# A hybrid decoder block on one core: five edits at the seams between its stages

## The reference

```python
z = rms_norm(h, norm_attn_g[i]) @ w_in[i]
y_attn = dilated_attention(q, k, v, rel_bias)
y_sgu = spatial_gating(z[..., o_g:o_s], ...)   # gelu, layer norm per group, causal 128x128 product, gate
y_ssm = s5_ssm(z[..., o_s:], ...)              # y = gelu(Re(C x) + D u); y * sigmoid(y @ glu_w + glu_b)
mix = concatenate([rms_scale(y_attn), rms_scale(y_sgu), rms_scale(y_ssm)], axis=-1) * branch_norm_g[i]
h = h + mix @ w_out[i]
h = h + conv_ffn(rms_norm(h, norm_ffn_g[i]), ...)   # up (width 5632), causal conv of 3, gelu(gate) * val, down
gate = sigmoid(rms_norm(h, norm_ple_g[i]) @ ple_w_gate[i])
h = h + gate * (p[i] @ ple_w_proj[i])
return rms_norm(h, final_norm_g)
```

## Time and profile before

| | |
|---|---|
| median of 3 runs | 2675.37 us (2674.75 to 2676.18) |
| profiled execution | 2676.85 us, span of its records 2675.3 us |
| mean granted PE clock | 0.973 of full |
| busy: PE, DVE, ACT, POOL | 95%, 67%, 51%, 31% |
| DMA | 420.97 MB, mean 157 GB/s |

### The profile page before, as it was taken

How to read it: one execution, slowest core, us unless ns; L and a number is a source line. 1 busy time by engine, 2 the same in 40 slices (tenths; PEclk the granted TensorE clock), 3 DMA queues, 4 the chain that set the end, 5 groups by cost and what they waited for, 6 DMA issues and landing times. The chain is left out here.

```text
span 2675.3 us, 38121 instructions
## 1 busy us (share of the span) xinstructions
PE 2532.1 (95%) x13395; PEld 2169.0 (81%) x13395; DVE 1794.4 (67%) x3337; ACT 1352.9 (51%) x2431; POOL 828.5 (31%) x625
## 2 busy tenths in 40 slices
PE   7999999999976899699999989999999999999998
PEld 6989979999965788488888868888888877887876
DVE  1113287777775776699999966879889975563333
ACT  4343424666645666455555546545555553444444
POOL 4454554655521111246555530002122210000000
PEclk9999999999987899799999999999999999999999
DMA  6675466788653454244444577543333336763221
GB/s 219 187 217 177 160 185 166 175 182 182 143 139 127 136 174 171 65 136 155 157 154 162 176 257 263 194 144 100 101 103 111 103 126 228 283 222 114 79 73 48
DMA packets 317450, 420.97 MB, mean 157 GB/s; under 512 B 31073, under 2 KB 229025, under 8 KB 312522
## 3 DMA queue, kind: packets, MB, share of 16 engines
q1 hardware_dynamic: 292090, 332.68, 41.4%
q0 software_dynamic: 25184, 86.01, 8.6%
HBM read 298.59 MB, written 124.16 MB: 158 GB/s over the span
## 5 line engine op out<-in xcount | busy, mean ns | idle before, releaser
L2834 PE MATMUL ffn_bank<-ffn_x,ffn_ring 128*128 128x512 f32 x704 | 278.1, 395 | 17.2 <-DVE ffn_strips L2632 8.9
L2836 PE MATMUL ffn_bank<-ffn_x,ffn_ring 128*128 128x512 f32 x704 | 277.2, 394 | 0.0
L2835 PE MATMUL ffn_bank<-ffn_x,ffn_ring 128*128 128x512 f32 x704 | 277.2, 394 | 0.0
L2908 POOL DMA_DIRECT2D ffn_act<-ffn_late x154 | 85.7, 558 | 476.1 <-DVE ffn_late L2664 445.4
L1203 POOL TENSOR_TENSOR in_w_lo<-in_w,in_w_hi 128x2048 fp32r<-128x2048 f32 x36 | 168.1, 4670 | 173.5 <-ACT in_w_hi L1071 173.5
L2834 PE MATMUL ffn_bank<-tail_shared,ffn_ring 128*128 128x512 f32 x528 | 206.3, 391 | 9.1 <-DVE ffn_ring L2607 7.5
L633 ACT ACTIVATE att_exps<-att_scores,att_part 128x256 f32<-128x256 f32 (+1 forms) x384 | 153.0, 454 | 105.1 <-DVE att_part L601 104.3
L2836 PE MATMUL ffn_bank<-tail_shared,ffn_ring 128*128 128x512 f32 x528 | 205.9, 390 | 0.0
L2431 ACT COPY ffn_strips<-ffn_bank 128x512 f32<-128x512 f32 x176 | 103.5, 588 | 147.6 <-PE ffn_bank L2836 147.6
L2648 DVE SCALAR_TENSOR_TENSOR ffn_strips<-ffn_strips,ffn_taps 128x512 f32<-128x512 f32 x176 | 144.6, 822 | 43.4 <-ACT ffn_strips L2446 43.4
L2834 PEld LDWEIGHTS ffn_bank<-ffn_x,ffn_ring 128*128 128x128 f32 x704 | 134.0, 190 | 49.0 <-issue 13.1
(11 more groups left out here) (441 smaller groups left out, 7369.3 us busy)
## 6 DMA issues: line engine op xcount, KB each, us to landing
ffn_w<-in_ffn_w_up SPq DMA_DIRECT2D x88, 512.0 KB, 4.8
ffn_act<-ffn_late POOLq DMA_DIRECT2D x154, 256.0 KB, 2.3
in_w<-in_w_in SPq DMA_DIRECT2D x36, 1024.0 KB, 6.6
ffn_a_raw<-ffn_act SPq DMA_DIRECT2D x77, 256.0 KB, 3.5
ffn_a_raw_later<-ffn_act SPq DMA_DIRECT2D x77, 256.0 KB, 4.4
ffn_w<-ffn_down_sums SPq DMA_DIRECT2D x16, 1024.0 KB, 5.1
ffn_w<-in_ffn_w_down SPq DMA_DIRECT2D x12, 1024.0 KB, 5.8
ffn_pieces<-in_ffn_w_down POOLq DMA_DIRECT2D x44, 256.0 KB, 3.6
```

Of the source, the lines that this page charges most:

```text
L2834: pe.matmul(out[:, :], hi[:, k], x_hi[kind][:, k], start=(k == 0 and fresh), stop=False, skip_group_check=not fresh)
L2835: pe.matmul(out[:, :], hi[:, k], x_lo[kind][:, k], start=False, stop=False, skip_group_check=not fresh)
L2836: mm = pe.matmul(out[:, :], lo[:, k], x_hi[kind][:, k], start=False, stop=(k == KH - 1), skip_group_check=not fresh)
```

## The change

1. `project_in`: the six bias bands are issued as before. Of the first head's twelve loads, the first half (six of 256 KB) is spread as four after block 29's work and two after block 30's, and the second half is cut in two parts of six smaller loads (128 KB each), spread over blocks 30, 31 and 32. The attention stage waits for 18 loads instead of 12.
2. `state_space`: the gate product `y @ glu_w + glu_b` is split by its contraction. The first half, with the bias written by a one-row matmul, is done in two batches of four banks, before q=4 and before q=6; ACT copies the banks to SBUF (`keep_first_glu`), DVE adds them to the second half later. `turn_y(0)` moves from q=6 to q=4. GpSimd multiplies three of the eight units (1, 3, 5). The load of mixing's row tile 0 is issued before the last store.
3. `mix_and_project`: ACT and DVE split weight chunk 0 ahead of waiting for row tile 0. In the opening step, `gate_product(3)` goes behind both products of tile 1, the turn of tile 2 behind it, and `gate_product(4)` from behind the products of tile 1 to behind the first products of tile 2.
4. `feed_forward`: the gain vector is loaded by SP near the end of the mixing stage. On ACT, PE and DVE the startup's pieces stand in another order, the second row group's turns have other banks, the copies of the first two products stand earlier, and the taps' turn and copy later.

The cut diff:

```diff
-                    load_first_head(0, units_to[G // 2 * NBLK] - 1)
+                if B == (G - 1) * NBLK + 2:
+                    load_first_head(0, 0, 4, units_to[G // 2 * NBLK] - 1)
+                if B == (G - 1) * NBLK + 3:
+                    load_first_head(0, 4, 6, units_to[G // 2 * NBLK] - 1)
+                    load_first_head(1, 0, 2, units_to[(G - 1) * NBLK] - 1)
+                if B == (G - 1) * NBLK + QK // WIDE:
+                    load_first_head(1, 2, 6, units_to[(G - 1) * NBLK] - 1)
                 if B == (G - 1) * NBLK + QK // WIDE + 1:
-                    load_first_head(1, units_to[(G - 1) * NBLK + QK // WIDE + 1] - 1)
+                    load_first_head(2, 0, 6, units_to[(G - 1) * NBLK + QK // WIDE] - 1)
             head_ahead.stored_counts = [stores_through(u) for u in range(U - RING, U)]
...
+    EARLY_AT, LATE_AT, EARLY_BANKS = Q // 2, Q - 2, 4
+    POOL_GATES = (1, 3, 5)
...
+                    if (h, l) == (HM - 1, L - 4):
+                        sp.wait_ge(stored[0], L // 4 * DMA)
+                        sp.dma_start(ahead.row0[:, heads * HEAD + GW:], mix[0:P, :]).then_inc(ahead.row0_loaded, DMA)
...
+            for n in POOL_GATES:
+                h, l = divmod(2 * n, L)
+                pool.wait_ge(rooted, n + 1)
+                nc.gpsimd.tensor_tensor(Y[:, h, l:l + 2, :], Y[:, h, l:l + 2, :], gate[:, h, l:l + 2, :], ALU.mult).then_inc(pool_out_ready, 1)
...
+            def first_glu_products(first):
+                for b in range(first, first + EARLY_BANKS):
+                    for i in range(2):
+                        n = 2 * b + i
+                        out = bank[b % EARLY_BANKS][:, i * W:(i + 1) * W]
+                        pe.matmul(out, ones[0:1, :], glu_b[0:1, :], start=True, stop=False)
+                        mm = pe.matmul(out, yT[:, 0, n * P:(n + 1) * P], glu_w[:, 0, :], start=False, stop=True)
+                    mm.then_inc(early_done, 1)
+
             for q in range(Q):
                 if q == MASK_AT:
                     turn_masks()
-                if q == Q - 2:
+                if q == EARLY_AT:
                     turn_y(0)
+                    pe.wait_ge(glu_loaded, 2 * DMA)
+                    pe.wait_ge(ones_ready, 1)
+                    pe.wait_ge(yT_copied, 4)
+                    first_glu_products(0)
+                if q == LATE_AT:
                     gate_product()
+                    pe.wait_ge(early_kept, EARLY_BANKS)
+                    first_glu_products(EARLY_BANKS)
                 pe.wait_ge(entry_ready, q // 2 + 1)
                 for h in range(HM):
...
-            pe.wait_ge(glu_loaded, 2 * DMA)
-            pe.wait_ge(yT_copied, 8)
+            pe.wait_ge(early_kept, 2 * EARLY_BANKS)
             for n in range(HM * L):
-                for k in range(2):
-                    mm = pe.matmul(bank[n // 2][:, (n % 2) * W:(n % 2 + 1) * W], yT[:, k, n * P:(n + 1) * P], glu_w[:, k, :],
-                                   start=(k == 0), stop=(k == 1))
+                if n % 4 == 0:
+                    pe.wait_ge(yT_copied, 4 + n // 4 + 1 if n < 2 * EARLY_BANKS else 8)
+                mm = pe.matmul(bank[n // 2][:, (n % 2) * W:(n % 2 + 1) * W], yT[:, 1, n * P:(n + 1) * P], glu_w[:, 1, :], start=True, stop=True)
...
+            def keep_first_glu(first):
+                for b in range(first, first + EARLY_BANKS):
+                    act.wait_ge(early_done, b + 1)
+                    nc.scalar.copy(glu_sums[:, 2 * b:2 * b + 2, :], bank[b % EARLY_BANKS].rearrange("p (l w) -> p l w", l=2)).then_inc(early_kept, 1)
...
+            sp.dma_start(rows_ahead.gain[:, :], rows_ahead.gain_src.rearrange("(k p) -> p k", p=P), allow_slow_non_contiguous=True).then_inc(rows_ahead.gain_loaded, DMA)
...
                         products(i, j, 1)
                         turn(i, 1)
                         gate_product(i, 2)
+                        continue
+                    if opening and j == 1:
+                        products(i, j, 1)
                         gate_product(i, 3)
+                        turn(i, 2)
                         continue
+                    if opening and j == 2:
+                        gate_product(i, 4)
                     if j + 1 < RING or not last:
                         turn(i, j + 1)
                     products(i, j, 1)
...
+            split_operand(0, 0)
             for k in KEEP_ORDER[:2]:
                 keep_first_group(0, k)
-            split_operand(0, 0)
+            round_second_group(0, 0)
             for k in KEEP_ORDER[2:]:
                 keep_first_group(0, k)
-            split_second_group(0, 0)
+            round_second_sum(0, 0)
+            round_second_group(0, 1)
             split_operand(0, 1)
-            for k in range(1, KH):
-                split_second_group(0, k)
-            for j in range(2, 4):
-                split_operand(0, j)
-            for n in range(3):
-                split_sums(0, n)
-                split_operand(0, 4 + n)
+            round_second_sum(0, 1)
+            round_second_group(0, 2)
+            keep(0, 0, 1)
+            round_second_sum(0, 2)
+            round_second_group(0, 3)
+            split_operand(0, 2)
+            round_second_sum(0, 3)
+            split_operand(0, 3)
+            split_sums(0, 0)
+            split_operand(0, 4)
+            split_sums(0, 1)
+            keep(0, 0, 5)
+            split_operand(0, 5)
+            split_operand(0, 6)
+            split_sums(0, 2)
             split_operand(0, 7)
             act.wait_ge(taps_ready, 1)
...
-                    if kind in (1, 5, 6, 4):
+                    if kind in (6, 4) or kind in (1, 5) and (h or f):
...
             split_operand(0, 0)
-            split_second_group(0, 0)
+            for k in range(2):
+                split_second_group(0, k)
             split_operand(0, 1)
-            dve.wait_ge(taps_turned, 1)
-            nc.vector.tensor_copy(taps[:, :, :], bank[3][:, 0:N_TAPS * 2 * F].rearrange("p (n f) -> p n f", f=2 * F)).then_inc(taps_ready, 1)
-            for k in range(1, KH):
+            for k in range(2, KH):
                 split_second_group(0, k)
             for j in range(2, 4):
                 split_operand(0, j)
-            for n in range(3):
-                split_sums(0, n)
-                if n < 2:
-                    split_operand(0, 4 + n)
+            split_sums(0, 0)
+            split_operand(0, 4)
+            split_sums(0, 1)
+            split_operand(0, 5)
+            split_operand(0, 6)
             sum_weights(0, 1, 0)
             sum_weights(0, 1, 1)
-            for j in range(6, SLOTS):
-                split_operand(0, j)
+            split_sums(0, 2)
+            split_operand(0, 7)
+            dve.wait_ge(taps_turned, 1)
+            nc.vector.tensor_copy(taps[:, :, :], bank[TAP_BANK][:, 0:N_TAPS * 2 * F].rearrange("p (n f) -> p n f", f=2 * F)).then_inc(taps_ready, 1)
             for s in range(2):
...
-                    if h == 0 and j == 2:
-                        pe.wait_ge(taps_ready, 1)
                     multiply(h, j)
                     if h == 0 and j == 0:
                         turn(0, 1, 1)
-                        turn_taps()
-                    if h == 0 and j == 1:
                         turn(0, 1, 2)
                         turn(0, 1, 3)
+                    if h == 0 and j == 1:
+                        turn_taps()
...
-            pool.dma_start(g_cols[:, :], gain.rearrange("(k p) -> p k", p=P), allow_slow_non_contiguous=True).then_inc(gain_loaded, DMA)
```

78 lines of the change are left out of this document (50 added, 28 removed).

## The result

The changed kernel took 2686.5 us (median of 6 runs, 2678.5 to 2690.0) against 2675.1 (6 runs, 2673.9 to 2679.0): slower by 11 us; the ratio on record is 1.0037, interval 1.0023 to 1.0051 (the quotient of the two medians is 1.0042). The forecast was 2669.5, in a range of 2659.5 to 2680.0. The profiled execution took 2687.36, span 2685.8.

A forecast was written before the change was run, and what follows sets the result against it. TensorE was taken as the bound, working 2532.1 of 2675.3 us. Terms −5.2 − 0.3 + 0 + 6.6 − 7.0 = −5.9 from the median 2675.37 gave 2669.5 us, range 2659.5 to 2680.0.

The forecast's parts named there:

- Part 2: State space, first half of the gate product early, batches of 7.0 us: gain 0.3, bounds loss 2 to gain 1.5.
- Part 1: In-projection, head prefetch spread so PE no longer waits for block 31's weights: gain 5.2, bounds 2.5 and 5.9.
- Part 3: Mixing, weight chunk 0 split before the first row: 0, at most 0.4 gained.
- Part 4: Mixing, gate products of tiles 3 and 4 later, delaying the other engines' chain: loss 6.6, bounds loss 9 to gain 2.7.
- Part 5: Feed-forward start, gain vector requested earlier and startup reordered: gain 7.0, bounds 4 and 14.
- Rival D: Mixing, gate 4 behind tile 2's products costs more, middle 13.5, so the kernel is slower: 2682 us, 15%.
- Rivals B and C: B: feed-forward start gains 14, 2662.5, 10%. C: block 32's weights late, feed-forward gains only 4.1, 2675, 19%.
- Rival A: Mixing reorder works as it looks, gaining 2.7 instead of losing 6.6: 2660.2 us, 14%.

The follow-up runs named there:

- 128-row: Changed kernel with the bias matmuls over 128 rows of 1/128 instead of one row: 2667.3 us, ratio 0.9969.
- zero-filled runs: Changed kernel with mixing's old opening order and bias matmuls over 128 rows, row 0 of the ones tile ones, the others zeros: 2660.9 us, ratio 0.9933.
- 64-row run: Changed kernel with mixing's old opening order and bias matmuls over 64 rows of 1/64: 2666.0 us, one execution.

## Why the prediction was wrong

- **Part 2, the failed step: "7.0 us a batch".** I priced the eight bias matmuls of a batch at 0.44 us, from the row of gate matmuls over 128 rows, and drew no bound for their being over one row. A batch measured 15.5: 3.0 for the other row count (10.0 at full clock), 5.5 for the clock that fell in it, and some 2.3 more at half clock behind it, in q=4 and q=6. Twice that is 21.6 of the 21.9 us between 110.1 and 88.2. That the row count is the cause is shown by the 128-row and zero-filled runs; that its pitch is a cost by itself by the 64-row run; why the clock falls is not shown beyond that. The range given for this part, a loss of 2 to a gain of 1.5, was made of the tail alone. The rest of it was low on the good side: 2.8 gained, not 0.3. Of the 3.8 us that the port could cost DVE's tail, 0.5 came.
- **Part 1** was right: 5.7 for 5.2. Block 32's weights went at 378.68 (378.3 said) and cost next to nothing.
- **Part 3** was right: with the old opening order mixing takes 236.3 against 236.0.
- **Part 4** was right in mechanism and size, 8.0 for 6.6. The first wait was 9.5 instead of 8, since tile 1's products ran at full clock throughout and ended 1.3 sooner, while tile 2's low parts started as late as before. Counted from mixing's first turn, tile 3's products started 6.0 later than before (6.2 said), and the half clock behind the second wait cost 1.6, where the sum has 0.4. That gate 4 behind tile 2's products moves the chain is shown by moving it (−4.8), that the order is a loss by undoing it (−8).
- **Part 5** was right in mechanism, low in size: 10.9 for 7.0, and 5.6 to 12.7 in the profiled executions of the kernels that keep this part whole. The vector was 3 to 4, as said; the order gave about 4.5, where I left 2.9 to it.
- **Rival D** had the right sign and a wrong place: mixing never lost more than 9. That its 2682 lies near the measured 2686.5 is luck.
- **Rivals B and C** did not come: the in-projection kept its 5.7, and the feed-forward gained neither 14 nor only the vector's 4.1.
- **Rival A** is refuted: tile 2's low parts do not come sooner when PE is free sooner.
